# An opening that builds H by chunk pairs and computes two gate units, in a hybrid SSD and attention kernel

## The reference

```
sh, sc, ... = split(silu(c) @ w_ada + b_ada)            # adaLN, for latent and for context tokens
h   = rmsnorm(x) * norm1_w * (1 + sc) + sh              # "H"
z, xbc, dt = split(h @ w_in)                            # z: 2048 wide, xbc: 3072, dt: 64
xbc = silu(conv5(xbc) + b)                              # centred depthwise convolution, 5 taps
dt  = softplus(dt + dt_bias)
y   = scan forward and backward over (xbc, dt), 4 groups of 8 heads, chunks of 128, + x * d_skip
out = rmsnorm(y * silu(z)) * gnorm_w @ w_out            # then x = x + gate * out
```

## Time and profile before

| | us |
|---|---|
| median of 3 runs | 1353.47 |
| lowest and highest | 1351.91 and 1355.84 |
| span of the profiled execution | 1352.0 |
| PE busy | 1195.1 (88% of the span) |
| DVE busy | 914.0 (68%) |
| ACT busy | 591.0 (44%) |
| POOL busy | 91.5 (7%) |

### The profile page before, as it was taken

How to read it: one execution, slowest core, us unless ns; L and a number is a source line. 1 busy time by engine, 2 the same in 40 slices (tenths; PEclk the granted TensorE clock), 3 DMA queues, 4 the chain that set the end, 5 groups by cost and what they waited for, 6 DMA issues and landing times.

```text
span 1352.0 us, 20115 instructions
## 1 busy us (share of the span) xinstructions
PE 1195.1 (88%) x7100; PEld 690.1 (51%) x7100; DVE 914.0 (68%) x1419; ACT 591.0 (44%) x1023; POOL 91.5 (7%) x105
## 2 busy tenths in 40 slices
PE   5849898998989599799999999997989967799997
PEld 2424454454544344334444444444855536688886
DVE  3676767857666589898887886746347656756654
ACT  3644453744656442243333342222335534566642
POOL 0004014050040000000000000000000000000000
PEclk8778889998899799899999999998999987899998
DMA  9211111121111416625565554440321101455552
GB/s 381 99 59 63 63 63 62 35 89 62 63 63 63 155 51 230 217 112 198 186 221 191 208 194 164 159 136 32 125 94 62 62 32 65 150 190 189 207 192 97
DMA packets 24238, 171.84 MB, mean 127 GB/s; under 512 B 2688, under 2 KB 2688, under 8 KB 5504
## 3 DMA queue, kind: packets, MB, share of 16 engines
q1 hardware_dynamic: 18288, 128.23, 26.1%
q0 software_dynamic: 5184, 37.75, 7.8%
q10 hardware_dynamic: 720, 5.24, 1.0%
HBM read 170.17 MB, written 1.05 MB: 127 GB/s over the span
## 4 chain that ended last, share of the span: by engine, by line
PE 71%; DVE 16%; ACT 4%; issue 4%; DMA 2%; POOL 1%; DVEq 1%; SPq 0%; ACTq 0%; POOLq 0%
PE bank L1421 19%; PE bank L1422 18%; PE bank L1423 18%; DVE arena L944 2%; DMA arena<-wada 2%; PE bank L1747 1%; DVE arena L830 1%; PE bank L1613 1%; PE bank L1602 1%; PE bank L1761 1%; DVE wl L800 1%; PE bank L1448 1%; DVE arena L877 1%; PE bank L1734 1%; PE bank L1736 1%
## 5 line engine op out<-in xcount | busy, mean ns | idle before, releaser
L1421 PE MATMUL bank<-hh,wh 128*128 128x512 f16 (+1 forms) x1136 | 395.3, 348 | 47.6 <-ACT arena L429 28.9
L800 DVE SCALAR_TENSOR_TENSOR wl<-raw,wh 128x1024 f16<-128x1024 f32 x224 | 266.3, 1205 | 206.8 <-ACT wh L389 205.7
L1422 PE MATMUL bank<-hl,wh 128*128 128x512 f16 (+1 forms) x1136 | 394.4, 347 | 0.0
L1423 PE MATMUL bank<-hh,wl 128*128 128x512 f16 (+1 forms) x1136 | 393.8, 347 | 0.0
L389 ACT ACTIVATE wh<-raw 128x1024 f16<-128x1024 f32 x224 | 229.1, 1043 | 281.7 <-PE bank L1423 210.8
L1421 PE MATMUL bank<-arena,wh 128*128 128x512 f16 (+1 forms) x544 | 181.5, 334 | 10.9 <-DVE wl L800 3.7
L1421 PEld LDWEIGHTS bank<-hh,wh 128*128 128x128 f16 x1136 | 113.1, 100 | 151.7 <-issue 66.8
L1422 PE MATMUL bank<-arena,wh 128*128 128x512 f16 (+1 forms) x544 | 181.3, 333 | 0.0
L1423 PE MATMUL bank<-arena,wl 128*128 128x512 f16 (+1 forms) x544 | 181.3, 333 | 0.0
L830 DVE SCALAR_TENSOR_TENSOR arena<-arena,araw 128x1024 bf16<-128x1024 f32 x144 | 167.6, 1219 | 0.2
L1423 PEld LDWEIGHTS bank<-hh,wl 128*128 128x128 f16 x1136 | 112.9, 99 | 94.8 <-issue 8.0
(11 more groups left out here) (214 smaller groups left out, 1344.3 us busy)
## 6 DMA issues: line engine op xcount, KB each, us to landing
raw<-wgu SPq DMA_DIRECT2D x44, 1024.0 KB, 4.8
arena<-wadaT POOLq DMA_DIRECT2D x36, 1024.0 KB, 5.1
raw<-wdn SPq DMA_DIRECT2D x16, 896.0 KB, 4.7
raw<-wxg SPq DMA_DIRECT2D x12, 1024.0 KB, 5.0
arena<-wada SPq DMA_DIRECT2D x8, 1024.0 KB, 18.0
raw<-wz SPq DMA_DIRECT2D x8, 1024.0 KB, 4.7
raw<-wout SPq DMA_DIRECT2D x8, 1024.0 KB, 4.8
raw<-wdn SPq DMA_DIRECT2D x8, 1024.0 KB, 4.9
```

The lines of the kernel that those rows point to most:

```text
L800: ve.scalar_tensor_tensor(wl[:, u.slot, a:b], raw[:, u.slot, a:b], WS, wh[:, u.slot, a:b], ALU.mult, ALU.subtract).then_inc(lo_done, 1)
L1421: pe.matmul(o, wh[:, u.slot, wsl], ahi[:, k, t0:t1], start=st, stop=False)
L1422: pe.matmul(o, wh[:, u.slot, wsl], alo[:, k, t0:t1], start=False, stop=False)
L1423: i = pe.matmul(o, wl[:, u.slot, wsl], ahi[:, k, t0:t1], start=False, stop=en)
```

## The change

The H of layer 0 is built in four pairs of chunks. SP loads x in two halves ahead of `keep`, then the adaLN units as pairs of one scale and one shift unit (4 and 0, 5 and 1, 6 and 2, 7 and 3), each pair giving the columns of two chunks. PE takes two pairs ahead of the first gemm step and the others between its steps, into banks 2 and 3 and into columns of banks 4 and 7 in turn. DVE works out each pair's columns in three instructions ahead of its chunks.

Three tiles of group 0 (2, 3 and 4) get padded buffers of their own, in the memory of x, which is free once the norm is multiplied. Two gate units (6 and 7) are computed in the opening, behind the running sums of dt; their SiLU lies in x's memory too, till the end of the scan. x is loaded again from HBM at the end of the last group, on ACT's queue. The last group has three gate units, and the hooks of four units are spread over these three.

```diff
@@ sync
-            sp.dma_start(x[:, :, :], xT).then_inc(in_x, 16)
-            for n in range(6):
-                load_first(n)
+            for h in range(2):
+                sp.dma_start(x[:, 4 * h:4 * h + 4, :], xT[:, 4 * h:4 * h + 4, :]).then_inc(in_x[h], 16)
+            sp.dma_start(kp[:, :], keep).then_inc(in_kp, 16)
+            load_first(4)
+            load_first(0)
             load(Unit(U_SSD0), wxg[0, :, 0:2048])
             sp.dma_start(dtraw, wdt).then_inc(in_dt, 16)
-            load_first(6)
-            load_first(7)
+            for n in range(1, 4):
+                load_first(4 + n)
+                load_first(n)
...
+            for k, z in enumerate(Z_FIRST):
+                load(Unit(U_ZF + k), wz[z])
@@ scalar
+            def evac_first(u, tile, b):
+                act.wait_ge(unit_done, u.half + (UD + 2))
+                if tile == 5:
+                    act.wait_ge(conv_ok, 2 + 2)
+                act.activation(first_pre(tile)[:, :, 2:258], GB[b][:, :]...).then_inc(pre_ok, 1)
+            def z_first(k, banks):
+                act.wait_ge(unit_done, Unit(U_ZF + k).half + (UD + 2))
+                for m in range(2):
+                    act.activation(zp[:, 2 * k + m, :], banks[m][:, :], ACT.Silu, ...).then_inc(zp_ok, 1)
...
-            act.wait_ge(mod_ok, 1)
-            for k in range(KC):
+            for k in range(4):
                 hi0(k)
+            ada0_out(2)
+            hi0(4)
+            hi0(5)
+            ada0_out(3)
+            hi0(6)
+            hi0(7)
...
             silu_xbc(0, 0)
+            evac_first(u.plus(1), 2, 2)
+            evac_first(u.plus(1), 3, 3)
+            cvt(u.plus(3))
...
-            silu_xbc(0, 2)
-            silu_xbc(0, 3)
+            evac_first(u.plus(2), 4, 0)
+            evac_first(u.plus(2), 5, 1)
+            cvt(u.plus(4))
             act.wait_ge(at_mm, 1)
...
+            silu_xbc(0, 2)
+            silu_xbc(0, 3)
+            z_first(0, GB[2:4])
+            cvt(u.plus(5))
+            silu_xbc(0, 4)
+            z_first(1, (YB, AB))
+            silu_xbc(0, 5)
...
                 square_z(7)
+                act.dma_start(x[:, :, :], xT).then_inc(in_x_again, 16)
@@ vector
+            def columns0(p):
+                ...
+                ve.wait_ge(a0_mm, p + 1)
+                step(ve.tensor_tensor(wsc[:, ks, :], ab[:, 0:2], wide(b_scale), ALU.add))
+                step(ve.tensor_tensor(wsc[:, ks, :], wsc[:, ks, :], wide(nw16), ALU.mult))
+                ve.scalar_tensor_tensor(wsh[:, ks, :], ab[:, 2:4], AS, wide(b_shift), ...).then_inc(mod_ok, 1)
...
             group(NG - 1, Unit(U_TAIL), False)
+            gate(2)
+            gate(3)
+            gate(4)
             add_z(4)
             add_z(5)
-            gate(3)
-            cvt(Unit(U_OUT))
+            cvt_half(Unit(U_OUT + 1), 0, 0, UF // 2)
             add_z(6)
-            gate(4)
             add_z(7)
...
+            ve.wait_ge(in_x_again, 16)
@@ tensor
             for k in range(KC):
+                if k in (2, 4):
+                    ada0(k + 2)
+                    ada0(k + 3)
+                    ada0_turn(k // 2 + 1)
                 pe.wait_ge(h_ok, k + 1)
...
             i.then_inc(at_mm, 1)
+            pe.wait_ge(pre_ok, 4)
+            gemm(Unit(U_ZF), [(0, GB[2][:, :]), (1, GB[3][:, :])], H, range(KC), 0, KC - 1)
+            pe.wait_ge(at_rest, 2)
+            gemm(Unit(U_ZF + 1), [(0, YB[:, :]), (1, AB[:, :])], H, range(KC), 0, KC - 1)
...
+                if not more:
+                    spread = [{} for _ in range(3)]
+                    for k in range(4):
+                        for j, hook in hooks[k].items():
+                            at_ = (8 * k + j) * 3 // 4
+                            spread[at_ // 8].setdefault(at_ % 8, []).append(hook)
...
-                for k in range(4 if more else 5):
+                for k in range(4 if more else 3):
```

More of the change, by code:

```diff
@@ L320, in build, with first_pre @@
         HN = {0: 0, 2: 1, 3: 2, 4: 3}
+        def first_pre(tile):
+            return px[:, tile - 2] if 2 <= tile < 5 else pre[:, tile % 2]
         block = ctx.enter_context(nc.Block())
@@ L560, in _, with ada0_out @@
                 act.activation(sq[:, k % 2, :], x[:, k, :], ACT.Square).then_inc(sqd, 1)
[L562 to L568 removed]
+            def ada0_out(p):
+                for j in range(2 * p, 2 * p + 2):
+                    act.wait_ge(a0_part, j + 1)
+                    act.activation(apart4[:, j, :], GB[2 + j % 2][:, 0:UN], ACT.Copy).then_inc(a0_out, 1)
             act.wait_ge(eps_ok, 1)
             root(0, D, 0)
[L571 to L572 removed]
             act.wait_ge(in_kp, 16)
@@ L900, in _ @@
             ve.memset(s2w, 0.0).then_inc(s2z_ok, 1)
+            nw16, b_scale, b_shift = small[:, 16:24], small[:, 24:32], small[:, 32:40]
+            ve.wait_ge(in_col, 16)
+            ve.tensor_scalar(nw16, cc("n1w", 0, KC), AS, None, ALU.mult)
+            ve.tensor_scalar(b_scale, cc("bada", KC, 2 * KC), 1.0, None, ALU.add)
+            step(ve.tensor_scalar(b_shift, cc("bada", 0, KC), AS, None, ALU.mult))
             ve.wait_ge(sqd, 1)
@@ L929, in _, with conv_tile @@
             cvt(Unit(U_SSD0 + 1))
-            def conv_tile(g, tile):
+            def conv_tile(g, tile, src=None):
+                src = pre[:, tile % 2] if src is None else src
                 n = g * 6 + tile
@@ L1081, in group @@
                     conv_tile(g + 1, 2)
-                else:
-                    gate(1)
                 from_state(g, 1)
-                cvt(u.plus(3))
+                if more:
+                    cvt(u.plus(3))
                 half_chunk(g, 2, 0)
@@ L1091, in group @@
                 else:
+                    gate(1)
                     add_z(2)
@@ L1095, in group @@
                     conv_tile(g + 1, 4)
-                else:
-                    gate(2)
                 from_state(g, 2)
                 from_chunk(g, 2)
+                if not more:
+                    cvt(u.plus(3))
                 half_chunk(g, 3, 0)
                 off(g, 3)
-                cvt(u.plus(4))
+                if more:
+                    cvt(u.plus(4))
                 half_chunk(g, 3, 1)
@@ L1481, in _ @@
             ssum(0, 0)
+            pe.wait_ge(s2_ok, 2)
+            ada0(0)
+            bcast(0, 0)
+            ada0(1)
             ada0_turn(0)
             ada0(2)
-            bcast(0, 0)
-            for a in range(3, ADA_FIRST):
-                ada0_turn(a - 2)
-                ada0(a)
-            ada0_turn(ADA_FIRST - 2)
-            ada0_turn(ADA_FIRST - 1)
+            ada0(3)
+            ada0_turn(1)
             u = Unit(U_SSD0)
@@ L1597, in within @@
                         pe.wait_ge(yb_ok, g * NCH + (c + 1))
+                    if c == 0 and hq == 0:
+                        pe.wait_ge(zp_ok, 4)
                     for h in range(4):
@@ L1659, in group @@
                          None]
+                if not more:
+                    spread = [{} for _ in range(3)]
[3 more added lines that the diff above has]
+                            spread[at_ // 8].setdefault(at_ % 8, []).append(hook)
+                    hooks = [{j: (lambda run=run: [hook() for hook in run]) for j, run in h.items()} for h in spread]
                 both = [(0, GB[0][:, :]), (1, GB[1][:, :])]
                 pe.wait_ge(pre_ok, g * 6 + 6)
-                for k in range(4 if more else 5):
+                for k in range(4 if more else 3):
                     if more:
```

151 lines of the change are left out of this document (79 added, 72 removed).

## The result

The changed kernel takes 1328.81 us (median of 4 runs, 1327.14 to 1331.08) against 1353.66 us (1351.91 to 1355.84), a ratio of 0.9818 with a 95% interval of 0.9804 to 0.9832: 24.9 us less. The forecast was 1332.

What follows compares the result with a forecast made beforehand. PE, busy for 88%, was taken to bound the last group and to idle in the opening and tail. Opening 9.2, tail 9.6 and hooked part 3.5 make 22.3, less 1 for handoffs: 1353.5 - 21.3 = 1332, range 1324 to 1341.

Steps and rivals of the forecast that it cites:

- Head: Up to dt's products: x earlier and columns in pairs bring the first gemm step near 31.8; gain 5.9, 5 taken.
- the walk: The prediction's step-by-step count of engine times through the changed kernel, giving 5.9 in the head and 5.3 in the hooked part.
- Convolutions: From dt's product to group 0's transposes: DVE's waits for ACT go, PE is busy throughout; gain 4.2 us.
- half-clock rival: In the head, adaLN steps between gemm steps keep the half clock: 0.4 instead of 5, 1336.6; chance 0.21 with late steps.
- Last group, hooked part: One gate unit's matmuls (10.4 us) go from the hooks, but PE's waits grow to 10.0: gain 5.3, 3.5 taken.
- the last group stays PE's: Rival in the last group: round trips are shorter than counted, so it gives 10.4, not 3.5: 1325; chance 0.11.
- Last group, tail: Behind the hooks the fifth gate unit goes, leaving 12.0 us on DVE against 21.6: gain 9.6.
- Second fetch: x loaded again at about 448, needed only for the first w_out residual some 40 us behind: cost 0.
- Sum: Whole kernel: 9.2 + 9.6 + 3.5 = 22.3 off the profiled 1352.0, less 1 us for handoffs: 1332.

Runs made afterwards that it cites:

- e10: The changed kernel with x fetched in one transfer behind `keep` instead of in two halves ahead of it: 1332.57 us, +3.7.
- e1: The changed kernel with all eight adaLN units and four turns ahead of the first gemm step, columns only then: 1332.84 us, +3.9.
- e7: The changed kernel with tiles 2 and 3 of group 0 in the two shared padded buffers again, 4 and 5 in their own: 1331.72 us, +2.8.
- e4: The changed kernel, its last group's three gate units without the product of high weights with H's low part (10.4 us of PE): 1323.73 us, -5.2.
- e3: The changed kernel without the second fetch of x and the wait for it: 1329.19 us, +0.3.
- e2: The changed kernel with the two gate units back in the last group (five there, none in the opening): 1340.54 us, +11.6.
- e8: e6 with tiles 2 to 4 of all groups put in the buffers in x's memory: 1313.82 us, -9.0 against e6.
- e11: e8 with ACT moving tiles 4 and 5 out ahead of the SiLU of tiles 2 and 3: 1303.30 us, 10.5 below e8.
- e5: The changed kernel with DVE's two sums into G for chunk 0 ahead of the second convolution or pair of squares: 1328.14 us, -0.8.
- e6: e5 with the last group's second gate SiLU before a pair of exps, a gate and squares inside DVE's last adaLN wait: 1322.85 us.

## Why the prediction was right

*Head.* Forecast: the first gemm step at 31.8, dt's product at 53.8, 5.9 by the walk and 5 taken. Found: 31.48 and 53.1, so 6.6 (59.66 in the earlier trace rows). The walk held step by step: steps 0 and 1 ended at 37.3 (forecast 37.1), steps 2 and 3 at 43.6 (43.8), and only the wait ahead of steps 6 and 7 didn't come. Behind the first step the clock came back no faster than in the earlier trace rows: steps 0 and 1 took 5.8 us, before 5.4. What the walk had wrong without harm is the clock of the adaLN work ahead of them, which was at 0.50 from 22 to 36 before and is 1.00 from 22 to 29; from 29 to 36 it is at the half clock too, behind a wait of 4.67. The steps between gemm steps ran at the full clock (1.93 for 32, and 0.98 from 36 to 50), so the half-clock rival fell. Two causes are shown: x's order is worth 3.7 (e10), the pairs 3.9 (e1). Together that is more than the 6.6, so the two don't simply add.

*Convolutions.* Forecast: PE busy throughout, at group 0 at 97.0, transposes at 103.3, DVE's tables at 99.2. Found: 97.4, 102.2 and 97.7. The term came out at 4.6 (11.2 less 6.6) against 4.2. That DVE would keep 3 us of slack nearly held (2.3). e7 prices the buffers in x's memory at 2.8, of which its profile shows 1.9 in the opening.

*Last group, hooked part.* Forecast 5.3 by the walk, 3.5 taken. The adaLN work ended at 442.83 and now at 427.35. From the transposes (370.69 and 356.56) that is 72.1 against 70.8, 1.4 less; from the group's first gemm step (363.08 and 349.67), which holds the same hooks, 79.8 against 77.7, 2.1 less. This is the term that was mis-sized, and only in size. The waits are as counted: from the transposes on PE idled for 4.8 us before and 9.3 now (forecast 5.0 and 10.0), with the two waits of 3 us at 3.05 and those of 1.7 and 1.0 at 1.30 and 0.74. What was too small is the price of the clock. It fell behind the first wait of 3.05, to 0.57 in the four us from 388 (4 x 0.43 = 1.7), and later the adaLN's small products took 4.39 instead of the 3.63 of before: together 2.5 of the 3.2 between walk and measurement. The other 0.7 I can't place. The rival "the last group stays PE's" fell with e4: a third of 10.4 us of matmuls came through.

The Trainium skill (TensorE: Matmul & The Clock Gate, HAM oscillation) tells of a matmul kernel that waits 3 to 5 us for a transfer in each turn of its loop and starts each turn at the half clock. The traces here agree for the waits of 4.36, each of which was followed by the half clock; of those from 2.1 to 3.1 us some were and others weren't.

*Last group, tail.* Forecast 12.0 us on DVE behind the last adaLN row against 21.6, so 9.6. Found: 427.47 to 438.94, 11.5 us; the same stretch was 21.6 by the earlier trace rows, so 10.1 less. DVE's rows are those counted: gates, squares and half a conversion, with no wait among them.

*Second fetch.* 0 forecast, +0.3 with an interval wider than that in e3.

*Sum.* 11.2 + 2.1 + 10.1 = 23.4 against 22.3 before the 1 us for handoffs. The remaining 0.8 of the 24.2 is 2.2 won in groups 0 to 2 by the clock less 1.4 lost behind the sum of squares, neither of which I call an effect. That the sum came so near is luck in part: the opening gave 2.0 more than the 9.2 taken for it, and the hooked part 1.4 less than its 3.5. Undone alone, the gate units' move is worth 11.6, the pairs 3.9, x first 3.7 and the buffers 2.8; as two of these overlap, their sum of 22.0 is no account of the 24.9.

What I had wrong and the result hid: I took e2's opening to come 8 us earlier without the gate units. It is 4.6 earlier, and moving them still pays, since the last group gives 12.2 for it. Groups 0 to 2, which the change leaves alone, hold 9.0 us more (e8) behind waits that the earlier trace rows show only by their clock.

## What to carry to other kernels

Move matmuls to a place where the matmul engine would idle, and price the move by what the engines that feed it must add there: 20.7 us of matmuls cost 4.6 in the opening and gave 12.2 in the last group. Where the hooks of a loop are spread anew, compare stretches that hold the same work. Where an engine waits once per loop turn, name the next limit before moving anything: here two limits less than 1 us apart gave 0.8 and 0 alone and 9.0 together. An engine that empties a bank should do that ahead of work that only its own next step needs, table loads above all.

## What the runs showed of the hardware

A wait of two to three us brought the clock down at some places and not at others, and its length didn't decide it. The same wait of 2.1 us, ahead of the same rows, was followed by 0.57 in one group and 1.00 in the next (above, behind the table). The stretch after behind the second wait of 3.05 us (columns as above):

```profile
403.40:409.00 5.60, 4.30 (x28) 2.38 (x29) 2.32 (x5) 5.57 (x10) 0.00 (x0) 1.00 0.00 0
```

It keeps the full clock, where the first wait of 3.05 us was followed by 0.57. In e8 the stretches behind 2.16 us in the last group and behind 2.70 in group 0:

```profile
394.70:400.70 6.00, 6.00 (x24) 2.63 (x25) 3.78 (x6) 3.04 (x10) 0.00 (x0) 0.72 0.00 0
156.10:160.10 4.00, 3.99 (x16) 1.62 (x17) 3.42 (x6) 3.97 (x7) 0.00 (x0) 0.57 0.00 0
```

The same wait in the last group, 2.17 us in e11, has the half clock from its first rows on:

```profile
390.48 0.57 PE L1657 MATMUL bank<-negm,idb 128*128 128x512 bf16 x1 [2.17 <-ACT arena L476]
390.84 0.63 PE L1661 MATMUL bank<-arena 96*128 96x128 bf16 x4
```

Behind each wait of 4.36 us, and behind each of 3.58 in e5 and e6, the half clock came within 2 us. What decides it for the shorter ones is not shown. A sum over waits of 2 to 3 us is therefore uncertain by some 2 us for each (86.5 against 84.4 for a group).

The clock also fell where PE didn't wait. In e11 the adaLN's small products (32 of 128x2) run from 250.97 for 4.04 us, and from 254 on PE is busy throughout at the half clock:

```profile
254.00:260.00 6.00, 6.00 (x25) 4.36 (x25) 1.30 (x5) 0.60 (x1) 2.50 (x2) 0.50 0.46 175
```

Behind the same products of group 2 after it was 0.51 (352 to 354), and in the last group it fell while they ran (4.39 us instead of 3.63).
